# Bias of v_B: added by VectorE out of PSUM in place of a product with a row of ones

## The reference

```python
x = _layernorm(x, ln_in_g, ln_in_b)                    # (16, 4096, 1024)
for l in range(2):
    h = x @ w_in[l] + b_in[l]
    q, k, v, g_a, u_b, v_b, g_b, r_a, r_b = _split_cols(h)
    y_a = _swa_sinks(q, k, v, sinks[l]) * silu(g_a)     # attention, window 128
    y_b = _chunked_sgu(gelu(u_b), gelu(v_b), vn_g[l], vn_b[l], w_s[l], b_s[l]) * silu(g_b)
    merged = sigmoid(r_a) * (y_a @ p_a[l]) + sigmoid(r_b) * (y_b @ p_b[l])
    x = _layernorm(ALPHA * x + merged @ w_out[l] + b_out[l], ln_g[l], ln_b[l])
```

## Time and profile before

| | |
|---|---|
| time, median of 3 runs | 3605.0 us (3602.7 to 3606.3) |
| profiled execution, its own time | 3604.8 us |
| its span on the slowest core (core 3) | 3603.3 us |
| spans of the eight cores | 3575.7 to 3603.3 us |
| mean granted TensorE clock, core 3 | 0.982 |
| TensorE matmuls | 3410.5 us busy, 18320 instructions |
| VectorE | 2318.8 us busy, 4993 instructions |
| ScalarE | 1824.2 us busy, 4065 instructions |
| GpSimd | 1401.2 us busy, 1295 instructions |

### The profile page before, as it was taken

The page is one execution under the profiler, slowest core; times in us unless marked ns, Lnnn a source line. Parts: engine busy times, 40 slices in busy tenths (PEclk is TensorE's granted clock), DMA queues, the critical chain, the costliest instruction groups (busy, mean ns, idle before and its releaser), DMA issues.

```text
span 3603.3 us, 61737 instructions; the slowest of 8 cores (3575.7 to 3603.3 us)
## 1 busy us (share of the span) xinstructions
PE 3410.5 (95%) x18320; PEld 1600.3 (44%) x18320; DVE 2318.8 (64%) x4993; ACT 1824.2 (51%) x4065; POOL 1401.2 (39%) x1295
## 2 busy tenths in 40 slices
PE   5778989999999999999999999999999999999997
PEld 2334444444444444444444444444444444444443
DVE  3445557666676676676776666766666667666667
ACT  3434445545555545655445654455654554555543
POOL 1324135442355331543334523444325542254343
PEclk9889999999999999999999999999999999999999
DMA  8784975538355344454454444544445534455433
GB/s 164 170 234 99 184 198 193 181 112 228 135 199 182 135 158 147 170 188 143 159 174 144 178 150 164 193 148 148 145 158 199 182 135 155 138 182 187 144 133 112
DMA packets 99112, 589.84 MB, mean 164 GB/s; under 512 B 11234, under 2 KB 11490, under 8 KB 42212
## 3 DMA queue, kind: packets, MB, share of 16 engines
q1 hardware_dynamic: 91012, 536.13, 42.2%
q0 software_dynamic: 7056, 49.29, 8.4%
q10 hardware_dynamic: 720, 0.46, 0.0%
HBM read 573.25 MB, written 61.87 MB: 176 GB/s over the span
## 4 chain that ended last, share of the span: by engine, by line
PE 87%; DMA 6%; DVE 3%; issue 1%; ACT 1%; POOL 0%; SPq 0%; DVEq 0%; POOLq 0%; ACTq 0%
PE ps L247 84%; DMA ring<-wpk 3%; PE ps L459 2%; PE ps L813 2%; DMA stg<-x 1%; DMA xres<-x 1%; DVE gbT L258 1%; ACT xT L255 1%; DMA tRb<-bs 1%; DVE nmx L780 0%; DVE ps L777 0%; DVE tRa L268 0%; DVE sm_i L268 0%; ACT L787 0%; POOL xres L258 0%
## 5 line engine op out<-in xcount | busy, mean ns | idle before, releaser
L247 PE MATMUL ps<-xT,ring 128*128 128x512 bf16 x8448 | 1967.7, 382 | 44.4 <-DMA ring<-wpk 25.0
L247 PEld LDWEIGHTS ps<-xT,ring 128*128 128x128 bf16 x8448 | 822.1, 98 | 1024.8 <-issue 105.5
L258 POOL TENSOR_TENSOR xres<-xres,gb 128x512 f32<-128x512 f32 x762 | 988.1, 1300 | 223.4 <-ACT xres L255 141.4
L258 POOL TENSOR_TENSOR Pq<-Pq,rcp 128x512 bf16<-128x512 bf16 x256 | 261.3, 1041 | 1010.2 <-DVE rcp L800 808.7
L787 ACT ACTIVATE Pq<-ps,nmx 128x128 bf16<-128x128 f32 x1024 | 371.8, 375 | 322.3 <-DVE nmx L268 320.3
L247 PE MATMUL ps<-ring,tRb 128*128 128x512 bf16 x2048 | 452.1, 381 | 19.0 <-DMA ring<-wpk 17.3
L247 PEld LDWEIGHTS ps<-ring,tRb 128*128 128x128 bf16 x2048 | 199.6, 98 | 257.9 <-issue 29.7
L247 PE MATMUL ps<-ring,xT 128*128 128x512 bf16 (+1 forms) x2048 | 304.3, 299 | 0.0
L255 ACT ACTIVATE xres<-xres,sm_p 128x1024 f32<-128x1024 f32 (+1 forms) x129 | 155.7, 1220 | 253.6 <-DVE sm_p L268 250.3
L258 POOL TENSOR_TENSOR sm_p<-sm_p,neghalf 128x2 f32<-128x2 f32 (+1 forms) x66 | 45.6, 691 | 577.9 <-DVE sm_p L262 574.8
L247 PE MATMUL ps<-gbT,ring 128*128 128x512 bf16 x1024 | 257.2, 379 | 0.0
(11 more groups left out here) (92 smaller groups left out, 3619.4 us busy)
## 6 DMA issues: line engine op xcount, KB each, us to landing
ring<-ws SPq DMA_DIRECT2D x371, 1024.0 KB, 5.8
ring<-wpk POOLq DMA_DIRECT2D x45, 1024.0 KB, 13.8
xres<-x SPq DMA_DIRECT2D x64, 512.0 KB, 6.8
stg<-x SPq DMA_DIRECT2D x60, 512.0 KB, 6.2
y<-xres SPq DMA_DIRECT2D x60, 512.0 KB, 4.8
ws<-ring SPq DMA_DIRECT2D x26, 1024.0 KB, 12.1
ring<-ws SPq DMA_DIRECT2D x28, 512.0 KB, 4.4
gb<-gbr SPq DMA_DIRECT2D x6, 512.0 KB, 13.6
```

The costliest lines, as they stand in the source:

```text
L247: P.add("pe", lambda e: e.matmul(out, lhsT, rhs, start=start, stop=stop), reads, writes)
L258: P.add(eng, lambda e: e.tensor_tensor(out=out, in0=in0, in1=in1, op=op), reads, writes)
```

## The change

The product with the row of ones and all that it needs (`row0`, the zeros of `vbb`) go. The bias is loaded into all 128 partitions and cast to bf16 there; VectorE adds it while it reads the bank, writes `vbg`, and the gelu runs in place on `vbg` in SBUF. The add is the bank's last reader.

```diff
     def setup_consts():
-        memset("dve", row0[:], 0.0, (("row0",),))
-        memset("dve", row0[0:1, :], 1.0, (("row0",),))
         for l in range(2):
...
-            memset("dve", vbb[l][:], 0.0, (("vbb", l),))
...
     def load_vbb(l):
-        dma("sp", vbb_f[0:1, l, :], vbb_d[l:l + 1, :], (), (("mixed", l),), ("c_vbb", l))
+        dma("sp", vbb_f[:, l, :], vbb_d[l].partition_broadcast(128), (), (("mixed", l),), ("c_vbb", l))
 
     def cast_vbb(l):
-        copy("dve", vbb[l][0:1, :], vbb_f[0:1, l, :], (("mixed", l),), (("vbb", l),))
+        copy("dve", vbb[l][:], vbb_f[:, l, :], (("mixed", l),), (("vbb", l),))
...
         for j in range(4):
             b = next_bank("W")
-            mm(ps[b][:], row0[:], vbb[l][:], True, False, (("row0",), ("vbb", l)), (("ps", b),))
             for kc in range(8):
-                mm(ps[b][:], xT[:, kc, j * 128:(j + 1) * 128], sl[:, kc, :], False, kc == 7,
+                mm(ps[b][:], xT[:, kc, j * 128:(j + 1) * 128], sl[:, kc, :], kc == 0, kc == 7,
                    RK(slot) + (("xT", kc),), (("ps", b),))
-            act(vbg[:, j, :], ps[b][:], AF.Gelu_apprx_tanh, (("ps", b),), (("vbg", j),))
+            tt("dve", vbg[:, j, :], ps[b][:], vbb[l][:], ALU.add, (("ps", b), ("vbb", l)), (("vbg", j),))
+            act(vbg[:, j, :], vbg[:, j, :], AF.Gelu_apprx_tanh, (("vbg", j),), (("vbg", j),))
```

More of the change, by code:

```diff
@@ L211, in build @@
     ident_bf = sb("ident_bf", [128, 128], BF16)
-    row0 = sb("row0", [128, 128], BF16)
     cs = sb("cs", [128, 2 * N_BIAS + 48 + 8])
```

## The result

The changed kernel takes **3700.3 us** in the profiled execution (a second one 3701.2), against 3604.8 before: ratio **1.027, 95% interval 1.024 to 1.029**. It is 95 us slower; predicted were 85, a time of 3690.

What follows compares the result with a forecast made beforehand. TensorE, busy 95% of the span, was taken as the bound, the removed products worth 27.7 us at most. Net delays reaching the fourth score product, 73 us, plus 12 us of clock, gave 3605 + 85 = 3690 us, range 3640 to 3735.

Steps and rivals of the forecast that it cites:

- round trip add, gelu, statistics: VectorE's strict queue on v tiles: each tile takes 2.4 us of round trip, against 1.73 us of TensorE.
- second of a round: Fourth score product: the late VectorE and ScalarE decide, +3.7 us in each of 7 stages; TensorE's wait grows to 4.6.
- Stage 15, step by step: Stage that also normalises input: TensorE waits 2.0, 1.0 and 0.5 us, net +2.6; ScalarE, with g0's Silu, +3.9.
- first of a round: Fourth score product: TensorE waits 3.33 us already, VectorE has no gaps, so +3.9 us in each of 7 stages.
- Stage 13: Stage with the bf16 residual copy: add 0 hides, two TensorE waits of 0.7 us, net +0.5; ScalarE's copy +3.7.
- The clock term: Longer fourth-score waits in 7 stages bring TensorE's lower clock, 1.7 us each, 12 us in all.
- Third and fourth: Fourth score product: gaps take up delay, leaving +0.5 us in 7 third stages and +3.3 in 5 fourth stages.
- Stage 7: TensorE's waits for weights behind the fourth score product take up the delay, so 0 us.
- The table load: ScalarE, ahead of gelu 0 in stage 15: its 1.28 us now comes behind add 0.
- Rival 1: Banks are free before u tile 3 and g0, the add hides: 27.7 us saved, 3577 us; chance 5%.
- Rival 2: Only TensorE's bank waits count, VectorE's and ScalarE's delay is taken up before the scores: 38 us, 3643; chance 22%.
- Rival 3: New short waits at u tile 3 and g0 also lower TensorE's clock: 20 us more, 3709 us; chance 18%.

Runs made afterwards that it cites:

- the copy without any bias arithmetic: The kernel before, product with the row of ones kept, with a VectorE copy from PSUM to SBUF ahead of each v gelu: 3699.6 us, ratio 1.024.
- the eight banks: The changed kernel with v, u and gate_B tiles over eight PSUM banks instead of five: 3707.5 us, ratio 1.029.
- no bias: The changed kernel without the add: bias of v_B left out, product gone, gelu reading PSUM as before: 3590.3 us, ratio 0.996.
- gelu table early: The changed kernel with a one-column gelu of constants ahead of the first v tile on ScalarE: 3697.0 us, ratio 1.025.
- before, copies late, Exp early: The kernel before, with ScalarE's input copies behind the fourth gate_A tile and a one-column Exp at the start of attention: 3577.7 us, ratio 0.992.

## Why the prediction was right, and where it was off

**The mechanism held.** The round trip add, gelu, statistics paces VectorE; the copy without any bias arithmetic shows the same loss, and the order of the queue alone takes most of it away. That the sum came so close is in part luck: the second of a round was put 4.5 us too high, the first 6.2, the third 2.3 and the fourth 5.2 too low.

**Stage 15, step by step** (predicted times moved by the 40.82 us). Add 0: 1813.27 predicted, 1813.14 measured. Gelu 0: 1815.22, 1815.14. Add 2: 1822.92, 1823.50. Add 3: 1825.62, 1826.01. Waits of TensorE: 2.0 + 1.0 + 0.5 = 3.5, measured 2.46 + 0.74 + 0.32 = 3.52. Silu of g0: 1834.3, 1834.77. What was 0.5 us short is one term: the input's statistics were taken at the 3.3 us of before, and took 3.98. Half of the difference is the small scale at their end (0.52 us, where before it was 0.17 to 0.21 in every such stage), half is a pause ahead of the second block of statistics for which the trace names no releaser. In ten of the other twelve such stages from stage 4 on the block takes 3.95 to 3.99 us as well, and there the small scale alone makes the difference, with 0.84 to 0.88 us. It explains 0.5 of the 0.9 us that a first of a round lost beyond the 3.9 predicted.

**Stage 13.** Gelu 3 ends at 1605.80, predicted 1569.9 + 35.72 = 1605.6; waits 0.86 + 0.57, predicted 0.7 + 0.7; the Silu of g0 4.0 us later, predicted 3.7.

**Second of a round, at the fourth score.** Here a step failed: that VectorE "has come without a gap from the Silus", so that "the late side decides" with +3.7 us and the wait grows to 4.6. It was 3.33: the products behind the Silus came 4.0 us later, the mask in front of the first Exp 2.8. VectorE had no gap, but a hidden reserve. The same instruction of stage 13, before:

```profile
1581.20 1.77 DVE L258 TENSOR_TENSOR gbT<-mixed,uT 128x512 bf16<-128x512 f32 x1
```

and after:

```profile
1620.81 0.68 DVE L257 TENSOR_TENSOR gbT<-mixed,uT 128x512 bf16<-128x512 f32 x1
```

That is 1.09 of the 1.2 us. GpSimd is busy with its own products at both places; what differs is which of the two started first. GpSimd's instruction before, and after:

```profile
1581.15 1.27 POOL L258 TENSOR_TENSOR xres<-xres,gb 128x512 f32<-128x512 f32 x1
...
1620.85 1.76 POOL L257 TENSOR_TENSOR xres<-xres,gb 128x512 f32<-128x512 f32 x1
```

Before, VectorE started 0.05 us behind GpSimd and took 1.77 us. After, it started 0.04 us ahead, took 0.68, and GpSimd's instruction took 1.76. A queue without idle time can still give time back where its instructions are stretched. The clock term held in kind (the lower level came, already at 3.33 us) and in size: in stage 13 4.4 us are 2.8 and 1.6. (The 3.69 us that the prediction gives for stage 8 before is the gap between weight loads; the matmul's own wait there is 3.22 us.)

**Third and fourth.** +0.8 for +0.5, and +3.6 for +3.3. Stage 7 was counted at zero, since two waits for weights should take the delay up. It lost 4.1 us. The two waits lie in stage 6, ahead of its scores, and I had put them one stage too late:

```profile
822.51 1.89 PE L247 MATMUL ps<-xT,ring 128*128 128x512 bf16 x8 [3.13 <-DMA ring<-wpk]
...
832.08 1.89 PE L247 MATMUL ps<-xT,ring 128*128 128x512 bf16 x8 [1.40 <-DMA ring<-wpk]
```

(before; stage 6 runs gelu 0 at 803.7 and its first Exp at 835.0). In stage 6 they did what was said of them: it lost 0.1 us. The 4.1 us are two fifths of the miss of 10. Stages 0 to 3 with the last came out at 1 us together, as said.

**The table load** (1.28 us in front of gelu 0) was written down as part of the delay. It is in the trace as predicted, but taking it out gave 4 us: in stage 15 its time was waited out beside GpSimd anyway. A delay that can be read from a row need not be a term of the sum.

**The gelu from SBUF** took 0.630 us, 0.032 more than from PSUM; 0.60 was taken. (The page "VectorE: DVE Perf Modes" of the Trainium skill, section "The TRN2 errata — SBUF-src ops pay a fixed extra latency per instruction", gave an estimate of 0.04: the trace agrees within 0.01.)

**Rival 1** (the add hides, 3577) falls. **Rival 2** (only the bank waits, 3643) falls to the eight banks: without those waits the time was 3707.5. That 27.7 us is the whole possible gain was right as a bound, and it was never reached in the order of the code as it is.

**Rival 3** (short waits cost the clock) holds for part of the stages, and its 20 us fall. Behind the 2.46 us of stage 15 the upper level stayed. In stage 12 of the change it did not:

```profile
1490.61 12.24 PE L246 MATMUL ps<-xT,ring 128*128 128x512 bf16 x48 [2.51 <-DVE vbg L257]
...
1490.58 0.99 PEld L246 LDWEIGHTS ps<-xT,ring 128*128 128x128 bf16 x6 [2.97 <-issue]
...
1494.04 0.15 PEld L246 LDWEIGHTS ps<-xT,ring 128*128 128x128 bf16 x1 [0.28 <-issue]
```

Six loads behind the wait still follow each other at 0.2 us, then they come every 0.43 us. The same happens in stages 8 (2.52 us) and 24 (3.00), so in three of the thirteen waits at u tile 3 from stage 4 on; over all eight cores it is 39 of 104, in stages 12 and 24 on every core and in 15 and 16 on none. It costs less than the 1.7 us of the rival: from the start of u tile 3 to the first spatial product it is 12.1 us where it is 11.26 in stages 15 and 16, and 0.3 to 0.4 us are left one gate_A tile later. The three stages lost 4.4 us each, no more than the other first ones (4.6 to 5.8), which fits VectorE and ScalarE being the late side there. (The page "TensorE: Matmul & The Clock Gate" of the Trainium skill, section "A second HAM failure mode: psum-queue depth-cycling", tells of such changes of the clock: at these waits the trace agrees in three of thirteen cases.)

**Stages 4 and 5** lost 5.8 and 6.1 us where their kind lost 4.2 to 5.1. The clock is most of it. In the kernel before, stage 4 is the one first of a round whose long wait left the upper level:

```profile
621.04 0.38 PE L247 MATMUL ps<-kpad,qT 128*128 128x512 bf16 x1 [3.40 <-DVE nmx L780]
...
621.48 1.42 PEld L247 LDWEIGHTS ps<-xT,ring 128*128 128x128 bf16 x8 [0.38 <-issue]
```

After, the wait there is 3.50 us and eight matmuls behind it run at the lower level, 1.7 us. In stage 5 it is eleven matmuls where the other second ones have seven or eight. Spread over the seven first ones, stage 4's 1.7 us are 0.24 of the 0.4 us of each that the input's statistics left open.

What stays open: the rest of that, under 0.2 us a stage, and why waits of the same length bring the lower level in one stage and not in another.

## What to carry to other kernels

Idle time on an engine doesn't make work that is moved to it free: what counts is what stands in front of it and behind it in that engine's queue. With all adds that free PSUM banks ahead of the statistics that wait for ScalarE, the loss of 95 us here becomes one of 9. Before an edit, look at what stands in front of the consumer on every engine, the next tile's conversions on ScalarE included; with the adds first, moving that work was worth another 44 us, more than the product that was removed. And a small VectorE instruction whose row was much longer than its minimum was waiting for GpSimd here, and that wait changes when anything ahead of it moves.

## What the runs showed of the hardware

- A VectorE addition over two columns takes 0.17 us, and up to 1.27 us (no bias) beside GpSimd's `tensor_tensor` of some 1.3 us; in stage 15 with the gelu table early two of them end within 0.1 us of GpSimd's instruction. With these additions on GpSimd the kernel is 42 us faster. The adds out of PSUM stayed at 676 to 693 ns all 128 times, GpSimd busy or not. The additions for v in the change:

```profile
L261 DVE TENSOR_SCALAR sm_v<-mv_v x64: 169/170/1176, 57.4 to 3599.7; 128x2 f32<-128x2 f32 x64
```

- The length of a wait on TensorE alone doesn't tell whether the lower clock level follows. It followed waits of 2.51, 2.52 and 3.00 us (the change, stages 12, 8 and 24), 2.55 (no bias, stage 13) and 1.73 (before, copies late, Exp early, stage 8), and not waits of 2.46 (the change, stages 15 and 16), 2.88 (the change, stage 7), 3.13 (before, stage 6) and 3.40 (before, stage 4). At the fourth score of the change, with waits of 3.22 to 4.79 us in the first and second of a round, it followed all fourteen times.
- Of two instructions of VectorE and GpSimd that start nearly together, the one that starts first kept its time and the other was stretched: 0.68 and 1.76 us, or 1.27 and 1.77 (stage 13, after and before).
- The table load starts when the wait of its instruction is over, not before (0.07 us behind add 0); a one-column activation of the same function ahead of the wait moves it.
